# Shared expert's down product moved into the first expert pair, one-hots ahead of the overflow list, and unread products in TensorE's idle times

## The reference, cut to what matters

```python
u = h @ w1 + b1; a, gt = split(u); u = a * sigmoid(gt)      # conv_module, layer 0
dw = depthwise_conv(u, 31 taps) + bdw
mix = silu(rms_norm(dw, gn)) @ w2 + b2
...
scores = sigmoid(x @ router_w)                              # moe: 64 experts, top 8 of 4 of 8 groups
wsel = scores of the chosen / their sum * 2.5
routed = sum over the chosen of wsel * (silu(x @ wg[e]) * (x @ wu[e])) @ wd[e]   # hidden width 256
out = routed + (silu(x @ sg) * (x @ su)) @ sd               # the shared expert
```

## Time and profile before

| | us |
| --- | --- |
| three runs: median, lowest, highest | 1323.28, 1322.66, 1323.49 |
| the profiled execution: time, span | 1324.85, 1323.0 |
| TensorE busy (share of the span) | 1263.2 (95%) |
| VectorE, ScalarE, GpSimd busy | 442.4, 324.3, 62.2 |
| first `conv_input` product | 38.61 |
| `project` in layer 0 starts | 131.23 |
| down product of the shared expert, layer 0 and layer 1 | 192.21, 836.94 |
| overflow ranks on VectorE, layer 0 | 204.34 to 209.48 |
| last pair's gate and up, layer 0 and layer 1 | 644.79, 1288.81 |

### The profile page before, as it was taken

One profiled execution on the slowest core, in us unless ns is written; L12 is line 12 of the kernel. 1 busy time (PEld: TensorE's weight loads), 2 busy tenths in 40 slices (PEclk: granted clock), 3 DMA queues, 4 the chain that ended last, 5 costly groups with the idle time before them and its releaser, 6 DMA issues.

```text
span 1323.0 us, 18761 instructions
## 1 busy us (share of the span) xinstructions
PE 1263.2 (95%) x6886; PEld 697.8 (53%) x6886; DVE 442.4 (33%) x1499; ACT 324.3 (25%) x711; POOL 62.2 (5%) x94
## 2 busy tenths in 40 slices
PE   5996999999999999999979898999999999999997
PEld 2773875454455455445444577644544544544544
DVE  1597172223222222222233544522222222222222
ACT  2376232112112212112130433121221221221211
POOL 0197000000000000000000000000000000000000
PEclk8897999999999999999979999999999999999998
DMA  9989798999999999999996538399999999999994
GB/s 362 383 306 369 297 354 336 419 421 420 419 420 421 421 420 420 421 420 420 377 413 283 231 156 332 151 421 419 420 419 420 420 421 420 421 421 421 420 420 185
DMA packets 84026, 497.47 MB, mean 376 GB/s; under 512 B 10681, under 2 KB 19553, under 8 KB 27648
## 3 DMA queue, kind: packets, MB, share of 16 engines
q1 hardware_dynamic: 83392, 496.47, 91.9%
q10 hardware_dynamic: 576, 0.22, 0.1%
HBM read 493.26 MB, written 3.41 MB: 375 GB/s over the span
## 4 chain that ended last, share of the span: by engine, by line
PE 84%; DMA 5%; DVE 5%; ACT 3%; issue 2%; SPq 1%; POOL 0%; POOLq 0%; ACTq 0%; DVEq 0%
PE ps L900 33%; PE ps L932 16%; PE ps L943 9%; PE ps L871 6%; PE ps L612 4%; PE ps L684 3%; DMA S<-in_exp_w_up_dram 3%; DVE ps L1488 3%; DMA ring<-in_conv_w_dram 2%; PE ps L817 2%; PE ps L585 2%; PE ps L918 1%; PE ps L600 1%; PE ps L855 1%; PE ps L910 1%
## 5 line engine op out<-in xcount | busy, mean ns | idle before, releaser
L900 PE MATMUL ps<-ring,xg 128*64 128x512 f32 x1344 | 296.5, 593 | 0.1
L900 PEld LDWEIGHTS ps<-ring,xg 128*64 128x64 f32 x1344 | 101.9, 137 | 189.1 <-issue 174.6
L900 PE MATMUL ps<-S,xg 128*64 128x512 f32 x704 | 154.9, 592 | 1.4 <-DMA S<-in_exp_w_up_dram 1.4
L932 PE MATMUL ps<-ring,W 128*64 128x512 f32 x672 | 153.5, 598 | 0.0
L1774 DVE TENSOR_TENSOR ypart<-ps,ypart 128x512 fp32r<-128x512 f32 x128 | 88.5, 692 | 179.6 <-ACT ypart L1330 179.6
L1763 DVE SCALAR_TENSOR_TENSOR vec<-silu_h,W,ps 128x256 f32<-128x256 f32 x64 | 30.8, 481 | 337.5 <-ACT silu_h L1324 337.5
L943 PEld LDWEIGHTS ps<-comb,ypart 128*128 128x128 f32 x1024 | 126.4, 190 | 18.6 <-issue 18.6
L943 PE MATMUL ps<-comb,ypart 128*128 128x256 f32 x1024 | 135.2, 285 | 0.0
L1319 ACT ACTIVATE xg<-ps 128x384 f32<-128x384 f32 x176 | 83.2, 491 | 171.7 <-PE ps L871 171.7
L1324 ACT ACTIVATE silu_h<-ps 128x256 f32<-128x256 f32 x64 | 24.6, 384 | 408.3 <-PE ps L900 408.3
L1330 ACT ACTIVATE ypart<-ps 128x512 fp32r<-128x512 f32 x128 | 76.4, 597 | 184.7 <-PE ps L932 184.7
(11 more groups left out here) (237 smaller groups left out, 1082.3 us busy)
## 6 DMA issues: line engine op xcount, KB each, us to landing
ring<-in_exp_w_gate_dram SPq DMA_DIRECT2D x86, 1024.0 KB, 17.3
ring<-in_exp_w_up_dram SPq DMA_DIRECT2D x86, 1024.0 KB, 19.4
ring<-in_exp_w_down_dram SPq DMA_DIRECT2D x86, 1024.0 KB, 19.0
S<-in_exp_w_gate_dram SPq DMA_DIRECT2D x44, 1024.0 KB, 17.8
S<-in_exp_w_up_dram SPq DMA_DIRECT2D x44, 1024.0 KB, 19.9
S<-in_exp_w_down_dram SPq DMA_DIRECT2D x44, 1024.0 KB, 19.7
ring<-in_ada_w_dram SPq DMA_DIRECT2D x26, 1024.0 KB, 21.1
S<-in_ada_w_dram SPq DMA_DIRECT2D x22, 1024.0 KB, 13.3
```

Of the source, the lines that this page charges most:

```text
L900: mm = pe.matmul(PGU[64 * b:64 * b + 64, :].rearrange("p (h f) -> p h f", h=2), xg[:, places[k][m], 64 * b:64 * b + 64], gate_up_of(w[b])[ ...
L932: mm = pe.matmul(bank[64 * b:64 * b + 64, :], hidT[:, j, 64 * b:64 * b + 64], down_of(w[b])[:, j, n * 512:(n + 1) * 512], start=(j == 0), ...
```

## The change

1. `shared_down()` moves from ahead of the gathers into pair 0, between `gate_up` and `hidden_t`; the list's product becomes `overflow_list()` behind the gathers. On VectorE `one_hots(0, 0)` and `slot_weights(0)` move ahead of the `h_lo` subtractions.
2. SyncE splits the load of `extra[1]`: gate and up once the shared hidden products are done (`sh_up`), down once the shared down product is done, which now stands behind the gate/up loads of pair 3. The first turn of the loading loop is written out for this.
3. `keep_clock(bank, n)`: n products of `ones` with the identity, 128 columns each, into a bank that nothing reads before it is written again. They stand between the ada units at the start (3 after each of units 3 to 7, 9 after the transposes), ahead of and behind `ada_transposes(1)` (18 and 9), and in layer 1 behind `sum_squares` ahead of the router (12).

```diff
+                sp.wait_ge(sh_up, 2 * l + 2)
+                load_weights(l, 5, extra[1], "gu", ld_gu_x[l][1])
-                sp.wait_ge(sh_done, l + 1)
-                load_extra(l, 1)
...
+                sp.wait_ge(pe_gu[l], 1)
+                for b in range(2):
+                    load_expert(l, 6 + b, b, "gu")
+                sp.wait_ge(sh_done, l + 1)
+                load_weights(l, 5, extra[1], "dn", ld_dn_x[l][1])
+                sp.wait_ge(pe_dn[l], 2)
+                for b in range(2):
+                    load_expert(l, 6 + b, b, "dn")
+                for half in range(1, 3):
+                    load_pair(half + 3, half, half + 1, 2 * half + 2, load_expert if half == 1 else load_expert_at)
+                with sp.Fori(1, N_DEEP) as it:
-                with sp.Fori(0, N_DEEP) as it:
...
+            def keep_clock(bank, n):
+                for _ in range(n):
+                    pe.matmul(bank[:, 0:P], ones, ident, start=True, stop=True)
...
-            ada_products(range(2, KC - 1), ps[0])
+            for u in range(2, KC - 1):
+                ada_products([u], ps[0])
+                if u >= 3:
+                    keep_clock(ps[2], 3)
...
             ada_products(range(KC - 1, KC), ps[0])
+            keep_clock(ps[2], 3)
             ada_transposes(0, ps[0])
+            keep_clock(ps[2], 9)
...
                     sum_squares(2, 7, 0, 6)
+                    pe.wait_ge(cv_in, 5)
+                    keep_clock(ps[3], 18)
                     ada_transposes(1, ps[1])
+                    keep_clock(ps[3], 9)
                     sum_squares(2, 7, 6, KC)
...
                     ada_products(range(3 * KC + 4, EARLY), ps[0])
+                else:
+                    keep_clock(ps[0], 12)
...
-                pe.wait_ge(rt_list, l + 1)
-                pe.matmul(ps[7][0:1, 0:MAXOVF], ubf[0:NE, 1, 0:1], ovl[:, :],
-                          start=True, stop=True).then_inc(rt_tab, 1)
+                def overflow_list():
+                    pe.wait_ge(rt_list, l + 1)
+                    pe.matmul(ps[7][0:1, 0:MAXOVF], ubf[0:NE, 1, 0:1], ovl[:, :],
+                              start=True, stop=True).then_inc(rt_tab, 1)
...
                     gate_up(i, t, PLACES[trio % 2], m, half, fill)
+                    if c == 0:
+                        shared_down()
...
-                shared_down()
                 pe.wait_ge(ht_done, l + 1)
                 pe.wait_ge(dve_g[l], 1)
                 for k in range(KC):
...
                     gather(0, k, (PG, PY, PT, PGU)[k % 4])
+                overflow_list()
...
                 dve.tensor_scalar(novb[:, :], ones[0:NE, :], novc[:, 4:5], None, ALU.mult).then_inc(rt_nov, 1)
+                one_hots(0, 0)
+                slot_weights(0)
                 for i in range(4):
...
-                one_hots(0, 0)
-                slot_weights(0)
```

More of the change, by code:

```diff
@@ L405, in load_expert, with load_extra @@
                 load_weights(l, e, ring[:, s, :], part, ld_gu[l][s] if part == "gu" else ld_dn[l][s])
-            def load_extra(l, b):
+            def load_extra(l):
                 for part, loaded in (("gu", ld_gu_x), ("dn", ld_dn_x)):
-                    load_weights(l, 4 + b, extra[b], part, loaded[l][b])
+                    load_weights(l, 4, extra[0], part, loaded[l][0])
             def expert_of(src, l, e):
@@ L473, in _ @@
                     load_shared(0)
-                    load_extra(0, 0)
+                    load_extra(0)
                     sp.wait_ge(pj_out, 4)
@@ L508, in _ @@
                     keep_y(1)
-                    load_extra(1, 0)
-                sp.wait_ge(sh_done, l + 1)
-                load_extra(l, 1)
+                    load_extra(1)
+                sp.wait_ge(sh_up, 2 * l + 2)
+                load_weights(l, 5, extra[1], "gu", ld_gu_x[l][1])
                 def load_pair(i, half, gu_before, dn_before, load):
@@ L1703, in _, with column, one_hots, slot_weights @@
                 dve.tensor_scalar(novb[:, :], ones[0:NE, :], novc[:, 4:5], None, ALU.mult).then_inc(rt_nov, 1)
+                def column(values, e):
+                    return values[:, e:e + 1] if type(e) is int else values[:, bass.ds(e, 1)]
+                def one_hots(t, buffer):
+                    for n in range(6):
+                        for g in range(G):
+                            ins = dve.tensor_scalar(hot[buffer][:, g, SLOTS * n:SLOTS * (n + 1)], iota,
+                                                    column(rank[:, g, :], 6 * t + n), None, ALU.is_equal)
+                    ins.then_inc(dve_g[l], 1)
+                def slot_weights(i):
+                    src = wt2[:, :, :, 2 * i:2 * i + 2] if type(i) is int else wt2[:, :, :, bass.ds(2 * i, 2)]
+                    dve.tensor_copy(wst, src).then_inc(dve_w[l], 1)
+                one_hots(0, 0)
+                slot_weights(0)
                 for i in range(4):
@@ L1727, in _ @@
                 shared_half(1)
[L1730 to L1745, removed]
                 def combine_copy(i, par):
```

## The result

| | before | after |
| --- | --- | --- |
| median of the runs, us | 1323.38 (1322.66 to 1323.82, 4 runs) | 1314.65 (1311.12 to 1315.97, 4 runs) |
| ratio | | 0.993, 95% interval 0.9911 to 0.995 |
| profiled execution: time, span, us | 1324.85, 1323.0 | 1311.12, 1309.2 |

The change makes the kernel 9.3 us faster (6.6 to 11.8 by the interval). Two further comparisons on other chips gave 0.9929 (0.9916 to 0.9943) and 0.9923 (0.9909 to 0.9936).

The account below looks back on a forecast made before the run. Bound by TensorE and DMA, both full in the expert loop, with TensorE's clock lost at the start and before the second projection. Terms 1.39 + 0.98 + 1.39 + 0.41 + 3.0 + 2.9 + 0.4 = 10.5 us; 1312.8 us, range 1309.5 to 1319.5.

Parts of the forecast that it names:

- The first chunk: Convolution's first output chunk: with the clock kept full by unread products, 7.2 us and not 10.21, 3.0 us earlier.
- The second projection: End of the tap stage: clock held by 18 and 9 products, projection starts at 128.3, not 131.23, 2.9 us.
- rival (a): Clock still lost at the start or before the second projection: 1315.7 to 1315.8, chance 0.17; in both 1318.7, 0.07.
- the rule on transposes: Transposes don't count as clock activity like products, so the four between the new products might still lose the clock.
- Shared product in pair 0: First expert pair: down product runs while hidden values are made; waits of 0.30 and 1.00 go, 1.39 us per layer.
- The cover on VectorE: One-hots ahead of the h_lo subtractions: VectorE ends at 191.3 against 191.75 for TensorE, 0.4 us of cover.
- The stream: Expert weight loads issued earlier: 7.25 - 2.5 - 1.3 = 3.5 us of lead, of which TensorE needs 2.4 and 1.8.
- end waits: Waits for the last pair's weights at the expert loops' ends go: 0.98 us in layer 0, 0.41 in layer 1.
- the 1.3 us for a dry queue: Pair 4's gate/up issued about when the load queue runs dry: 1.3 us off the lead for issue to first traffic.
- Rival (c): Stream, not TensorE, sets the loops' end, lead under 2.4 us: at worst 1.4 us less per layer, 1315.6, chance 0.12.
- Layer 1's router: 12 products in the 3.49 us wait ahead of it: its 32 records take 4.16 and not 4.58 us, 0.4 us.
- The sum: Whole kernel: all terms together 10.5 us, giving 1312.8 us; full sum within 1.3 us, chance 0.58.

Follow-up runs that it names:

- e_start: Kernel before plus only the start's unread products (threes behind units 3 to 7, nine behind the transposes): 1321.11 us, ratio 0.9983.
- e_part1: Changed kernel with all keep_clock calls taken out: 1318.28 us, ratio 0.997 against the kernel before.
- e_proj: Kernel before plus only the 18 and 9 unread products around ada_transposes(1): 1319.73 us, ratio 0.9972.
- v_next: Changed kernel plus 12 more unread products behind the sums that open layer 1: 1312.86 us, ratio 0.9925 against the kernel before.
- e_hotslate: Changed kernel with one-hots and slot weights back behind the table, list's product ahead of the gathers: 1320.49 us, ratio 0.9989 against the kernel before.
- e_oldload: Changed kernel with expert 5's load in one piece, after the shared down product, ahead of pair 3's gate/up: 1328.68 us, ratio 1.005 against the kernel before.
- e_part2: Kernel before plus all the unread products and nothing else: 1317.08 us, ratio 0.9959.
- e_nonine: Kernel before plus the start's threes, without the nine products behind the transposes: 1322.57 us, ratio 0.9997.
- after_again: The changed kernel, unchanged, measured once more: 1312.21 us, ratio 0.9929 against the kernel before.
- after_third: The changed kernel, unchanged, measured a third time: 1312.91 us, ratio 0.9923 against the kernel before.
- v_next_b: Same kernel as v_next, measured again beside the changed kernel on one chip: 1313.33 us, ratio 0.993 against the kernel before.

## Why the prediction was right, point by point

**The first chunk.** Forecast 3.0 us by a full clock from 21 us on; the chain has 3.02, and the windows from 24 to 45 us are at 1.00. That no transfer ends a wait up to 125 us held: the whole stage moved along. As an average the term is smaller, e_start's 2.2 us (1.1 to 3.4), and the profiled execution of before may well have had it above its average: the same chunk took 9.69 in e_part1 and 9.83 us in e_proj, which have nothing added there.

**The second projection.** Forecast at 128.3 in before's time; e_proj has 128.08 behind a start at 38.67. Forecast and ledger agree to 0.1 us, and e_proj's 3.7 us (2.5 to 4.9) hold it. What rival (a) starts from, a clock lost in this place, happened in v_next, but the 3 us that it takes off didn't follow: there the products behind the lost clock brought it back before the ada records. The four transposes between the products did no harm in any profile (1.00 in 109 to 131 us in after); what the rule on transposes would have cost here never showed. The products are a little dearer than forecast, 4.18 and 2.17 us for 18 and 9 and not 3.9 and 1.9. The waits still hid them: 0.66 us are left of the 4.63.

**Shared product in pair 0.** Forecast 1.39 us per layer, measured 1.8. The 0.30 and 1.00 us went; of the rest, 0.3 us is the start of the gathers and 0.1 the way from the transposes to pair 1 (4.88 us, was 4.99). The gathers start 3.37 us after the last hidden group's first record (182.19); in before that record is at 188.07, so they would start at 191.44, and I had 191.75. The cover on VectorE held, but by 0.1 us and not the 0.4 forecast (the h_lo subtractions end at 185.46, ahead of 185.56), and e_hotslate gives the worth of the early one-hots: 7.6 us.

**The stream.** This is the term that was mis-sized. Right was that the loop lives on the stream's lead: in e_oldload, with a stream that comes later, the loops wait although TensorE's path is the changed kernel's. Forecast was 3.5 us of lead and both end waits gone, 1.39 us. Measured at pair 4, whose second up load lands at 231.15 us (before: 239.48), the stream is 2.4 us earlier, counted from the second projection. What became of that at the loops' ends, in the profiles of either order of loads (without e_hotslate, whose pair 0 comes late; 0 where the profile has no wait):

| us | old order: before, e_part2, e_start, e_nonine, e_proj | new order: after, after_again, after_third, e_part1, v_next, v_next_b |
| --- | --- | --- |
| landing of the last pair's up load behind pair 1's start, layer 0 | 428.0, 427.3, 427.0, 427.3, 427.3 | 426.7, 427.2, 426.0, 426.7, 427.6, 426.6 |
| the same, layer 1 | 427.3, 426.9, 426.9, 426.8, 427.0 | 427.5, 426.8, 427.5, 427.2, 426.0, 426.2 |
| end waits, both layers together | 1.39, 0, 0, 0.18, 0.40 | 0.59, 0, 0.57, 0.29, 0.40, 0 |

On the mean the landings move up against pair 1 by 0.57 us in layer 0 and by 0.13 in layer 1, and pair 1 itself by 1.77: a stream 2.3 and 1.9 us earlier, not 3.5. The scatter between executions of one order, up to 1.6 us, is larger than the shift against pair 1. The end waits are 0.4 us on the mean in the old order and 0.3 in the new, so the term is worth about 0.1 us, not 1.39. I had counted the kernel's worst reading as its mean. The step that failed in the lead itself is the 1.3 us for a dry queue behind pair 4's issue. No row shows that figure, and what came in its place is a longer stretch at a reduced rate. Windows of it, after:

```profile
210.00:213.00 3.00, 3.00 (x16) 1.01 (x14) 0.58 (x2) 0.00 (x0) 0.00 (x0) 1.00 0.93 287
213.00:216.00 3.00, 3.00 (x15) 0.79 (x11) 0.00 (x0) 0.00 (x0) 0.00 (x0) 1.00 0.94 382
216.00:223.00 7.00, 7.00 (x49) 4.80 (x48) 2.19 (x7) 2.42 (x5) 0.00 (x0) 1.00 0.95 349
223.00:600.00 377.00, 376.80 (x2078) 186.80 (x2076) 98.52 (x345) 74.55 (x148) 0.00 (x0) 1.00 1.01 420
```

and the kernel before in its corresponding stretch, at full rate throughout:

```profile
216.00:219.00 3.00, 3.00 (x16) 0.99 (x14) 1.23 (x3) 0.60 (x1) 0.00 (x0) 1.00 1.03 426
222.00:229.00 7.00, 7.00 (x48) 4.72 (x46) 1.61 (x6) 1.82 (x4) 0.00 (x0) 1.00 1.01 420
```

Against 420 GB/s the after windows miss 133 x 3, 38 x 3 and 71 x 7 kB/us, together 1.0 MB or 2.4 us. By these numbers the lead is 7.25 - 2.5 - 2.4 = 2.35 us, the 2.4 that pair 4's landing shows. The stretch belongs to the new order: after_again has 322, 404 and 343 GB/s in the same windows, and e_proj, with the old order, 419 or more from 210 to 229 us. Why the rate falls is not shown; SyncE's rows have pair 3's two down loads issued from 209.18 us, ahead of the fall, so the queue wasn't simply empty. Rival (c) was the nearest to what happened, at a price of 1.3 us and not 2.8.

**Layer 1's router.** 4.17 us for 4.58: the 0.4 forecast.

**The sum.** Parts measured alone: 4.0 and 5.4 us, the whole 9.3 to 10.2 in three comparisons, forecast 10.5. By term, forecast and measured: the start 3.0 and 2.2, the second projection 2.9 and 3.7, the shared product in both layers 2.8 and 3.6, the end waits 1.4 and 0.1, the router 0.4 and 0.4. The mechanisms are those forecast but for the end waits. That the total came so near is in part luck: the shared product's 0.8 us more made up for most of the 1.3 that the stream didn't bring, and the first two terms are known to 1.2 us each.

## What to carry to other kernels

Filler pays where it ends right before dense work that it keeps fast, not where it merely fills: without the nine products in front of the loop, the others at the start brought nothing. Moving work ahead of a transfer-fed loop can cost more than it brings if loads that wait for that work come later by it (e_oldload); find the issue that gates the stream, split the load there, and price the stretch until the stream is at its full rate again by its rate in windows. And take the clock's losses and the small waits at a loop's end from several executions, since one profile can hold all of them or none.

## What the runs showed that I had not expected

A clock lost ahead of filler is not lost for the loop behind it (v_next: 0.54 in 112 to 116 us, 1.00 from 116 on). Gathers that started 3.2 us late made gate/up 4.7 us late, as they ran slow behind the wait (e_hotslate). The transfer rate fell to 287 GB/s for 3 us with a DMA share of 0.93, so a high share alone doesn't say that the stream runs at its 420. Unchanged code at the opening of layer 1 took 7.13 us in some executions and up to 10.19 in others. That is as much as the 2 to 3 us between most runs of one kernel, but no run ties the two together.
